# A two-block model on one core: the first mixer's value and gate columns in shared chunks, its long convolution divided anew among three engines

## What is computed

```python
def pool_conformer_mixer(h, w_in, pool_w, pool_scale, conv_w, conv_b, ln_g, ln_b, w_out):
    z = jnp.einsum("btd,de->bte", h, w_in)                 # 2048 -> 3072
    u_pool, v, gate = z[..., :1024], z[..., 1024:2048], z[..., 2048:]
    y_pool = multiscale_pool(u_pool, pool_w, pool_scale)   # windows of 2, 4, 8, 16 tokens, then a 256x256 product per group
    c = causal_depthwise_conv(v * jax.nn.sigmoid(gate), conv_w) + conv_b   # 31 taps per feature
    y_conv = jax.nn.silu(layer_norm(c, ln_g, ln_b))
    return jnp.einsum("bte,ed->btd", jnp.concatenate([y_pool, y_conv], axis=-1), w_out)
```

## Time and profile before

| | us |
|---|---|
| median of 3 runs | 2781.31 (2780.73 to 2781.59) |
| the profiled execution | 2780.84 |
| its span, first to last instruction | 2779.1 |

### The profile page before, as it was taken

How to read it: one execution, slowest core, us unless ns; L and a number is a source line. 1 busy time by engine, 2 the same in 40 slices (tenths; PEclk the granted TensorE clock), 3 DMA queues, 4 the chain that set the end, 5 groups by cost and what they waited for, 6 DMA issues and landing times.

```text
span 2779.1 us, 30965 instructions
## 1 busy us (share of the span) xinstructions
PE 2735.8 (98%) x12357; PEld 2262.7 (81%) x12357; DVE 1576.9 (57%) x1705; ACT 1299.6 (47%) x1649; POOL 309.2 (11%) x328
## 2 busy tenths in 40 slices
PE   8888999999999999999999999999999999999999
PEld 7677888888888888888888888888888888888887
DVE  4998654555445565555654554555556447654454
ACT  5665544444434454444454443444446447544342
POOL 2873100000000010000100000000011001100000
PEclk9999999999999999999999999999999999999999
DMA  6444555555555555555565555564555555455554
GB/s 234 139 159 139 197 185 193 189 206 176 196 188 182 196 177 201 194 195 188 178 208 191 182 182 184 195 208 171 191 189 176 198 181 166 164 207 197 187 182 152
DMA packets 259185, 515.58 MB, mean 186 GB/s; under 512 B 8114, under 2 KB 10724, under 8 KB 258532
## 3 DMA queue, kind: packets, MB, share of 16 engines
q1 hardware_dynamic: 259044, 513.60, 53.6%
HBM read 511.47 MB, written 2.10 MB: 185 GB/s over the span
## 4 chain that ended last, share of the span: by engine, by line
PE 90%; DVE 6%; issue 2%; POOL 1%; ACT 0%; DMA 0%; POOLq 0%; SPq 0%; ACTq 0%
PE bank L621 29%; PE bank L623 29%; PE bank L622 29%; DVE conv_out L1448 3%; DVE w_lo L607 3%; PE bank L667 2%; POOL acc L1617 0%; DMA w_raw<-in_ab_w_in 0%; POOL small L1611 0%; PE bank L798 0%; PE bank L856 0%; DVE x_res L1288 0%; DVE B_lo L1233 0%; DVE z L1464 0%; ACT w_hi L600 0%
## 5 line engine op out<-in xcount | busy, mean ns | idle before, releaser
L607 DVE TENSOR_TENSOR w_lo<-w_raw,w_hi 128x1024 fp32r<-128x1024 f32 x960 | 1180.6, 1272 | 699.1 <-ACT w_hi L600 693.6
L600 ACT ACTIVATE w_hi<-w_raw 128x1024 fp32r<-128x1024 f32 x960 | 978.2, 1058 | 622.9 <-PE bank L623 518.0
L621 PE MATMUL bank<-w_hi,A_lo 128*128 128x512 f32 x2432 | 958.2, 394 | 16.9 <-DVE w_lo L607 16.5
L623 PE MATMUL bank<-w_hi,A_hi 128*128 128x512 f32 x2432 | 949.7, 391 | 0.0
L622 PE MATMUL bank<-w_lo,A_hi 128*128 128x512 f32 x2432 | 949.0, 390 | 0.0
L621 PE MATMUL bank<-w_hi,B_lo 128*128 128x512 f32 x1408 | 553.3, 393 | 14.0 <-DVE w_lo L607 6.3
L621 PEld LDWEIGHTS bank<-w_hi,A_lo 128*128 128x128 f32 x2432 | 458.0, 188 | 115.8 <-DVE w_lo L607 23.5
L622 PE MATMUL bank<-w_lo,B_hi 128*128 128x512 f32 x1408 | 550.1, 391 | 0.0
L623 PE MATMUL bank<-w_hi,B_hi 128*128 128x512 f32 x1408 | 550.0, 391 | 0.0
L623 PEld LDWEIGHTS bank<-w_hi,A_hi 128*128 128x128 f32 x2432 | 457.8, 188 | 96.3
L622 PEld LDWEIGHTS bank<-w_lo,A_hi 128*128 128x128 f32 x2432 | 458.4, 188 | 92.7
(11 more groups left out here) (143 smaller groups left out, 827.9 us busy)
## 6 DMA issues: line engine op xcount, KB each, us to landing
w_raw<-in_ffn_w SPq DMA_DIRECT2D x256, 1024.0 KB, 5.4
w_raw<-in_w_in SPq DMA_DIRECT2D x88, 1024.0 KB, 5.1
w_raw<-in_sc_w_in SPq DMA_DIRECT2D x48, 1024.0 KB, 5.4
w_raw<-in_ab_w_in SPq DMA_DIRECT2D x24, 1024.0 KB, 5.2
w_raw<-in_ab_w_out SPq DMA_DIRECT2D x16, 1024.0 KB, 5.0
w_raw<-in_sc_w_out SPq DMA_DIRECT2D x16, 1024.0 KB, 5.7
w_raw<-in_w_out SPq DMA_DIRECT2D x16, 1024.0 KB, 5.3
w_raw<-in_w_proj_a SPq DMA_DIRECT2D x8, 1024.0 KB, 5.2
```

The costliest lines, as they stand in the source:

```text
L600: e.activation(w_hi[:, s % SPLIT_SLOTS, :], raw, ACT.Copy).then_inc(hi_made, 1)
L607: e.tensor_tensor(w_lo[:, slot, :], raw, w_hi[:, slot, :].bitcast(F32), ALU.subtract).then_inc(lo_made, 1)
L621: e.matmul(ps, lo[:, kt, tok], wh, start=first, stop=False)
L623: ins = e.matmul(ps, hi[:, kt, tok], wh, start=False, stop=last)
```

## The change

- Chunks 0 to 3 each take 256 value columns and the 256 gate columns that belong to them. A load of such a chunk is two DMAs with rows of 1 KB. At its end ScalarE makes the sigmoid of the gate half (act_gate), and VectorE multiplies the value half in the bank by the scale and the sigmoid (dve_gate). GpSimd's product goes. The transposes follow behind step 2 of the next chunk, steps 10, 18, 26 and 34, one bank each.
- The taps run from step 11 to 57. VectorE has the blocks 0, 2, 4, 6 and taps 15 to 30 of block 7, ScalarE blocks 1, 3, 5 and taps 0 to 14 of block 7. VectorE adds even and odd taps into two halves of PSUM bank 7 and joins them. ScalarE makes its products in pairs, and GpSimd adds a pair, 512 columns, to two sums in one instruction, and joins the two sums at the end of a block. There are two slots for pairs.
- Until the first mixer ends, three banks serve the rotating fills instead of four.
- The norm is applied by ScalarE (act_norm), with a bias that VectorE makes; so is the gain and bias before silu. Transposes, norm and silu lie one step earlier: 58, 59, 61, 62.

```diff
-        put(2 * j, w, 0, 16, D_POOL + j * CH, "A", 0, pre(0))
-        put(2 * j + 1, w, 0, 16, 2 * D_POOL + j * CH, "A", 0, pre(0))
+        for q in (2 * j, 2 * j + 1):
+            put(q, w, 0, 16, D_POOL + q * QUARTER, "A", 0, pre(0))
...
+EARLY_TAPS = 15
+DVE_TAPS = []
+for _b in (0, 2, 4, 6):
+    DVE_TAPS += [(_b, _k) for _k in range(CONV_K)] + [(_b, "join")]
+DVE_TAPS += [(7, _k) for _k in range(EARLY_TAPS, CONV_K)] + [(7, "join0"), (7, "join1")]
+ACT_TAPS = [(_b, _k) for _b in (1, 3, 5) for _k in range(CONV_K)] + [(7, _k) for _k in range(EARLY_TAPS)]
+TAP_FROM, TAP_TO = 11, 58
...
+        tap_sums = [bank[7][:, 0:TOK], bank[7][:, TOK:2 * TOK]]
...
+                pieces = [(col0, CH)] if c >= 4 else [(col0, QUARTER), (col0 + D_POOL, QUARTER)]
+                at_col = 0
+                for col, width in pieces:
+                    src = w[row:row + GK * P, col:col + width].rearrange("(k p) c -> p k c", p=P)
+                    e.dma_start(dst[:, :, at_col:at_col + width], src).then_inc(raw_loaded[slot], 16)
...
+        def act_gate(e, q):
...
+            for tt in tiles:
+                wait_chunk(e, q, tt)
+                e.activation(z[:, s, tt, QUARTER:], main_bank(q, tt)[:, QUARTER:], ACT.Sigmoid,
+                             scale=rs(0)[:, tt:tt + 1]).then_inc(gate_made(q, tt), 1)
...
+        def act_tap(e, b, k):
...
+            elif k == 1:
+                if b > 1:
+                    e.wait_ge(tap_added.sem, tap_added.of(b - 2, "join"))
+                e.activation(odd_taps, src, ACT.Copy, scale=w)
...
+        def act_norm(e, tt):
...
+            for h in two:
+                e.activation(z_flat[z_slot("n", tt)][:, h * CH:(h + 1) * CH], aux_bank("ln", tt, h), ACT.Identity,
+                             scale=cols(1, "root", "ln", tt), bias=cols(1, "ln_bias", tt)).then_inc(ln_made(tt, h), 1)
...
+        def dve_gate(e, q):
...
+            for tt in tiles:
+                e.wait_ge(gate_made.sem, gate_made.of(q, tt))
+                e.scalar_tensor_tensor(z[:, s, tt, 0:QUARTER], main_bank(q, tt)[:, 0:QUARTER], rs(0)[:, tt:tt + 1],
+                                       z[:, s, tt, QUARTER:], ALU.mult, ALU.mult).then_inc(dve_took(q, tt), 1)
...
+            else:
+                e.wait_ge(tap_done.sem, tap_done.of(b, k - 2))
+                e.scalar_tensor_tensor(out if b < 7 and k == CONV_K - 1 else sums, src, w, sums, ALU.mult,
+                                       ALU.add).then_inc(tap_done(b, k), 1)
...
+        def pool_add(e, b, m):
...
+            if (b, 2 * m + 1) in ACT_TAPS:
+                both = conv_out[:, b:9:8 - b, :]
+                e.tensor_tensor(both, both, taps.rearrange("p (k t) -> p k t", k=2), ALU.add).then_inc(tap_added(b, m), 1)
```

More of the change, by code:

```diff
@@ L137, in att_tasks, with taps_at, pool_adds @@
     return ATT_TASKS[int(ATT_RATE * step):int(ATT_RATE * (step + 1))] if 8 <= r < 14 else []
[L141 to L146, removed]
+EARLY_TAPS = 15
[5 more added lines that the diff above has]
+TAP_FROM, TAP_TO = 11, 58
+def taps_at(taps, s):
+    if not TAP_FROM <= s < TAP_TO:
+        return []
+    n, steps = len(taps), TAP_TO - TAP_FROM
+    return taps[n * (s - TAP_FROM) // steps:n * (s + 1 - TAP_FROM) // steps]
+def pool_adds(taps):
+    last = {1: CONV_K - 1, 3: CONV_K - 1, 5: CONV_K - 1, 7: EARLY_TAPS - 1}
+    for b, k in taps:
+        if k >= 2 and (k % 2 == 1 or k == last[b]):
+            yield b, k // 2
+        if k == last[b]:
+            yield b, "join"
 def pre_fills(p):
@@ L160, in aux_order @@
     yield from [("rows",)]
-    yield from [("vg", 0, h) for h in two]
-    yield from [("vg", 1, h) for h in two]
+    yield from [("vg", q) for q in range(4)]
     for j in two:
@@ L351, in build @@
         stat_made = signal("stat_made", [(p, tt) for p in range(5) for tt in tiles])
[L352 to L353 removed]
+        conv_fed = signal("conv_fed", [("vg", q) for q in range(4)] + [("cu", j, h) for j in range(NG) for h in two])
+        POOL_ADDS = list(pool_adds(ACT_TAPS))
+        tap_made = signal("tap_made", [add for add in POOL_ADDS if add[1] != "join"])
+        gate_made = signal("gate_made", [(q, tt) for q in range(4) for tt in tiles])
         pooled_made = signal("pooled_made", [(j, h) for j in two for h in two])
@@ L396, in build @@
         root_made = signal("root_made", ROOTS)
-        gated = signal("gated", [(j, tt) for j in two for tt in tiles])
-        tap_added = signal("tap_added", [tap for tap in TAPS if tap[2] >= 2 and tap[1] > 0])
+        tap_added = signal("tap_added", POOL_ADDS)
         gained = signal("gained", [(p, n, tt) for p in range(4) for n in range(NG) for tt in tiles])
@@ L496, in build @@
             load_row.append((c, i // STEPS_PER_LOAD))
+        LOADED = []
+        for n in range(LOADS):
+            before = LOADED[n - RAW_SLOTS] if n >= RAW_SLOTS else 0
+            LOADED.append(before + 16 * (2 if load_row[n][0] < 4 else 1))
         def at_chunk(c):
@@ new lines, in dve_tap @@
+        def dve_tap(e, b, k):
+            out, n = conv_out[:, b, :], tap_done.of(b, k)
+            if k == "join":
+                e.wait_ge(tap_done.sem, tap_done.of(b, CONV_K - 1))
+                e.tensor_tensor(out, tap_sums[1], out, ALU.add).then_inc(tap_done(b, k), 1)
+                return
+            if b == 7 and k in ("join0", "join1"):
+                part = int(k == "join1")
+                e.wait_ge(tap_done.sem, n - 1)
+                e.wait_ge(tap_added.sem, tap_added.of(7, "join"))
+                e.tensor_tensor(out, tap_sums[part], out, ALU.add).then_inc(tap_done(b, k), 1)
+                return
+            first = 0 if b < 7 else EARLY_TAPS
+            src, w, sums = conv_in[:, b, k:k + TOK], par_col(COL_CONV, 8 * k + b), tap_sums[(k - first) % 2]
+            if k == first:
+                e.wait_ge(conv_fed.sem, conv_fed.of("vg", b // 2))
+            if k < first + 2 and b > 0:
+                e.wait_ge(tap_done.sem, tap_done.of(b - 2 if b < 7 else 6, "join"))
```

214 lines of the change are left out of this document (113 added, 101 removed).

## The result

The changed kernel takes **2756.03 us** in the median of four runs (2754.54 to 2757.72), beside 2781.45 us for the kernel before in the same session (2780.73 to 2781.91): a ratio of 0.9909, with a 95% interval of 0.9892 to 0.9926. That is 25.4 us less; 27.0 less had been forecast (2754.3, range 2747 to 2771). The profiled execution is the slowest of the four, 2757.7 us with a span of 2756.0, so 23.1 us less than the profiled one of before.

A forecast was written before the change was run, and what follows sets the result against it. TensorE, busy 98% of the span, was taken as the bound, losing 39.7 us in the first mixer. Losses after of 1.8 + 5.3 + 2.5 + 1.0 + 2.0 = 12.6 leave 27.1 gained: median 2754.3 us, range 2747 to 2771.

The forecast's parts named there:

- The bound and its size: First mixer: TensorE bounds the kernel but waits for VectorE's w_lo; 39.7 us lost, the most the change can return.
- The taps at 0.41: VectorE's accumulating taps with sums in PSUM: no contention with GpSimd, 0.41 us each instead of 0.88 contended.
- The rival that ended slower: VectorE's 140 taps: writing PSUM is dear, at 0.88 us per tap 2797 us; chance 0.05.
- the one in which the taps still contend: VectorE's taps: PSUM operands don't free them from GpSimd, port times add up, 2773 us; chance 0.05.
- w_lo at 1.32: VectorE's w_lo, steps 11 to 57: 1.14 us plus 0.18 average wait for GpSimd, 62 us in all.
- GpSimd's 1.30 per pair: GpSimd's additions of 512 columns: 1.30 us each, 1.2 per step, so no bound.
- three split steps: ScalarE at chunk ends: stock of 8.2 us to cover the moved gate, of which 3 us are used.
- the block changes: Sign that the forecast is wrong: ScalarE's waits for GpSimd reach TensorE where the taps' blocks change.
- Step 50: TensorE's wait for B_lo of the second product: 1.8 us left of 3.97, 2.2 saved.
- The tail: End of first mixer, from step 58: silu half 6.9 us; waits 0.6, 1.6 and 3.1, together 5.3 us lost.
- The clock: TensorE after the 3.1 us wait before step 66: one step at the lower clock, 2.5 us lost.
- The start: First weight load split into two DMAs with 1 KB rows: 1.0 us lost, bounds 0.4 and 4 us.

The follow-up runs named there:

- E2: Kernel before, with each of GpSimd's tap additions cut to one column, all waits kept: 2748.6 us.
- E3: Changed kernel, with GpSimd's additions and joins cut to one column: 2750.4 us.
- E4: Changed kernel, with the taps spread over steps 17 to 57 instead of 11 to 57: 2756.3 us.
- E5: Changed kernel, with ScalarE's taps spread over steps 11 to 51 instead of 11 to 57, VectorE's unchanged: 2749.56 us, ratio 0.9888.
- E10: Changed kernel with ScalarE's taps ending at step 51, norm's product and silu's gain and bias on VectorE, and step 66's w_hi and w_lo queued earlier: 2747.94 us.
- E7: Changed kernel, with the norm's product and silu's gain and bias back on VectorE: 2755.27 us.
- E8: Changed kernel, with only silu's gain and bias back on VectorE, the norm staying on ScalarE: 2755.25 us.
- E11: Changed kernel, with GpSimd's addition of a pair as two of 256 columns instead of one of 512: 2756.37 us.

## Why the prediction came right, point by point

**The bound and its size.** 39.7 us of loss in the first mixer: some 33 of them are contention, by E2. Right, and the rest (start, step 50, tail) stood in the sum.

**The taps at 0.41.** 0.40 measured, 479 ns, from the one row of B_lo. The untested half, writing PSUM, costs nothing: 481 ns against 486 in E3 and E2. The rival that ended slower falls with it, as does the one in which the taps still contend. The Trainium skill (VectorE: DVE Perf Modes, The TRN2 errata) would have made each tap 65 ns longer from PSUM; no row here agrees with that for this operation, and the measurement decides.

**w_lo at 1.32.** Its starts stand 0.08 closer than its duration of 1.29, so 1.21 was paid. The price of a collision was right (1.22 to 2.13 us is 0.91; 0.92 had been worked out), but fewer w_lo pay it: GpSimd mostly comes second and pays instead.

**GpSimd's 1.30 per pair: the step that failed.** "1.2 of them per step are no bound" took the addition's own length, with the port's time on VectorE's side alone. For the stretch as a whole the conclusion holds all the same, by E4. It fails in the last steps. ScalarE has no stock of taps at the chunk's end, so the additions come in a queue from 186 us on; VectorE, catching up as well, issues a w_lo every 2.31 us, and each addition lands behind one and lasts 2.23 us. The five from 186.04 us on take 2.3 us each from start to start; the last, which met none, took 1.4. The prediction saw waits at the chunk ends "where ScalarE and VectorE wait for TensorE already" and put 2.0 us in the sum for what it couldn't place, up to 5; it was one wait of 4.04 us, in the place where conv_out is wanted, and E5 removed it by order alone. The stock of "three split steps" was counted for the weights and not for the taps queued behind the same copies. A join counted to the same delay: ScalarE stood 2.13 us for GpSimd at 183.65, which was among the signs that the prediction named against itself, at "the block changes".

The Trainium skill (SBUF — State Buffer, SBUF: two separate sides and Who interferes with whom) says that of a GpSimd instruction and a VectorE one in a two-port mode, or one with two SBUF inputs beside a GpSimd one that reads SBUF, the first to start holds the shared ports for the whole instruction and the other is blocked fully. The trace agrees for w_lo with its two SBUF inputs: 0.94 us lost by GpSimd's addition, 0.91 by w_lo. With this sentence applied to both engines the 2.24 us could have been worked out ahead.

**Step 50:** 1.93 us measured, 1.8 taken. **The tail:** the silu half takes 7.0 us (214.86 to 221.84), 6.9 taken; the waits before steps 64 and 66 are 1.04 and 2.81 us, 1.6 and 3.1 taken; the small wait at the norm didn't come, 0.6 taken, since TensorE itself was late. Reading the queue behind silu was right too: E10 shows that step 66 waited for its own w_lo, and E10's step was worth 1.05 us.

**The clock:** one slow step of 2.5 us taken, behind step 66's wait. Measured were slow matmuls behind three waits: some 1.7 us of loss after the one of 1.93 us, 2.4 after the one of 4.04, 1.2 after the one of 2.81. That term was mis-sized by some 3 us and differs from one execution to the next. With it fell the sign "clock near 1.00" up to 200 us: from 172 to 176 us it was 0.59.

**The start:** first matmul at 12.20 instead of 11.17 us, 1.0 taken. The size fits, the cause isn't shown: see below.

**The range and the place of step 66.** The cheap end was added up wrongly: with no lower clock, no unplaced wait and a start of 0.4 the terms leave 7.5 us of loss, so 32 us gained and 2749, not 34 and 2747. And "step 66 at about 228 us" is 215.1 plus all 12.6 us, though the slow step of 2.5 was put behind step 66; by the terms it was 225.2, and 230.48 was measured.

The errors went both ways: 2.0 for what had no place against 4.0, 2.5 against some 5.3 for the clock, 5.3 against 3.9 in the tail. By the rows the loss was 16.6 us, 15.4 up to step 66 and 1.2 behind it, against 12.6 in the sum, and the profiled execution lies the same 4 us above what the sum gives for it. The median is only 1.7 above the forecast, so part of the closeness is luck: the slowest execution was the profiled one. What carried the forecast, the taps at 0.40 us, was no luck.

## What to carry to other kernels

Where two engines share a port, look for operands that can lie in PSUM: one of two inputs there, and the output with it, freed 126 taps of all contention at no price in their own time, for one of the eight banks. Charge a collision to both engines, and sum the slower one with its dear price over the last stretch before a result is wanted, where its work queues up; over the whole phase the mean was far below that price. Work that feeds a slower engine belongs ahead of the copies with which the feeding engine waits for TensorE; that order was worth 6.5 us here and cost no instruction.

## What the runs showed of the hardware

The same wait of 1.93 us before step 50 was followed by slow matmuls in the changed kernel (granted clock 0.59 from 172 to 176 us) and by none in E5 (1.00 from 172 to 180). Of the twelve executions that waited 1.93 us there, five had seven or eight slow matmuls behind the wait (the changed kernel, E7 to E10) and seven had none. So the price of a short wait of TensorE is not fixed; here it lay between 0 and some 1.7 us. In the kernel's first step 6 to 12 matmuls of 12 were slow. Differences of this size lie within the 3 us by which single executions differ; that they make most of it isn't shown.

The changed kernel and the ten experiments with its split loads issue the same transfers at the start. Their first matmul came at 12.20 to 12.74 us in eight of these eleven executions, and at 10.96 to 11.16 in the other three (E7, E8 and E11). The kernel before and E2, without the split, stand at 11.17 and 11.73. So whether the smaller DMAs cost the 1.0 us is left open: the late start isn't in all of their executions, and a run with the first load in one piece wasn't made.

A single-column addition of GpSimd takes 0.19 us by itself, but 0.37 to 0.69 us in the mean of the groups of E2 and E3. It still waits for VectorE: in E3 one that starts at 99.48, with a w_lo from 99.30 to 100.52 beside it, lasts 1.08 us.
